# Sums over partitions with the stationary data in four column groups of 32

## The reference

```python
cs = jax.nn.silu(c)
for i in range(2):
    mod = (cs @ ada_w[i] + ada_b[i])[:, None, :]
    sh1, sc1, g1, sh2, sc2, g2 = jnp.split(mod, 6, axis=-1)
    h = rms_norm(x, norm1_g[i]) * (1.0 + sc1) + sh1
    x = x + g1 * mixer_i(h)          # 0: dilated attention, 1: S5 state space
    h = rms_norm(x, norm2_g[i]) * (1.0 + sc2) + sh2
    x = x + g2 * conv_ffn(h)
return rms_norm(x, final_norm_g)
```

## Time and profile before

| | |
|---|---|
| median of three runs | 2857.9 us |
| span of the profiled execution | 2854.5 us |
| TensorE busy with matmuls / weight loads | 97% / 88% |
| VectorE / ScalarE / GpSimd busy | 79% / 44% / 16% |
| mean granted TensorE clock | 0.985 |
| HBM traffic | 254 GB/s over the span |

### The profile page before, as it was taken

How to read it: one execution, slowest core, us unless ns; L and a number is a source line. 1 busy time by engine, 2 the same in 40 slices (tenths; PEclk the granted TensorE clock), 3 DMA queues, 4 the chain that set the end, 5 groups by cost and what they waited for, 6 DMA issues and landing times.

```text
span 2854.5 us, 52641 instructions
## 1 busy us (share of the span) xinstructions
PE 2761.2 (97%) x19980; PEld 2521.2 (88%) x19980; DVE 2249.6 (79%) x3003; ACT 1267.3 (44%) x1775; POOL 466.5 (16%) x461
## 2 busy tenths in 40 slices
PE   8799999999989999999999999989999999999998
PEld 3788888888889999999999998989878888888887
DVE  7887877777869988889888778987888875666655
ACT  1334444444434544434444334444355553455542
POOL 4061111011023111000111111234401110000121
PEclk9899999999999999999999999999999999999999
DMA  9989887787756888878888876768867766655563
GB/s 361 352 275 371 294 277 267 261 267 259 263 178 232 295 296 287 281 234 302 300 295 304 270 245 215 241 205 281 310 218 242 265 183 187 194 185 186 183 183 111
DMA packets 241693, 724.50 MB, mean 254 GB/s; under 512 B 50912, under 2 KB 59872, under 8 KB 240736
## 3 DMA queue, kind: packets, MB, share of 16 engines
q1 hardware_dynamic: 185184, 666.98, 68.9%
q10 hardware_dynamic: 56320, 54.93, 6.2%
HBM read 700.58 MB, written 25.43 MB: 254 GB/s over the span
## 4 chain that ended last, share of the span: by engine, by line
PE 87%; DVE 6%; issue 3%; DMA 2%; ACT 1%; POOL 1%; ACTq 0%; SPq 0%; DVEq 0%; POOLq 0%
PE proj L1827 31%; PE proj L1830 15%; PE proj L1832 11%; PE proj L1834 11%; PE proj L1833 11%; DVE acc L1025 2%; PE pmisc L1856 1%; PE proj L1826 1%; DMA raw<-in_w_in 1%; DMA ada<-in_ada_w 1%; DVE w_lo L1116 1%; PE ps L1915 1%; PE ps L1942 1%; PE proj L1915 1%; PE ps L2026 1%
## 5 line engine op out<-in xcount | busy, mean ns | idle before, releaser
L566 ACT ACTIVATE w_hi<-raw 128x1024 fp32r<-128x1024 f32 (+1 forms) x896 | 935.6, 1045 | 1411.3 <-PE proj L1834 580.0
L1116 DVE TENSOR_TENSOR w_lo<-raw,w_hi 128x1024 fp32r<-128x1024 f32 (+1 forms) x896 | 1107.1, 1236 | 467.1 <-ACT w_hi L566 462.3
L1827 PE MATMUL proj<-h_hl,w_hi 128*128 128x512 f32 x3232 | 1139.5, 400 | 6.5 <-DVE work L1294 3.9
L1830 PE MATMUL proj<-h_hl,w_lo 128*128 128x256 f32 x3030 | 851.5, 281 | 0.0
L1827 PEld LDWEIGHTS proj<-h_hl,w_hi 128*128 128x128 f32 x3232 | 599.0, 189 | 138.0 <-DVE work L1294 4.2
L1830 PEld LDWEIGHTS proj<-h_hl,w_lo 128*128 128x128 f32 x3030 | 574.6, 190 | 7.3
L1832 PE MATMUL proj<-h_hl,w_hi 128*128 128x256 f32 x1888 | 548.6, 291 | 30.0 <-DVE h_hl L1071 11.0
L1833 PE MATMUL proj<-h_hl,w_hi 128*128 128x256 f32 x1888 | 538.8, 285 | 0.0
L1834 PE MATMUL proj<-h_hl,w_lo 128*128 128x256 f32 x1888 | 538.6, 285 | 0.0
L1832 PEld LDWEIGHTS proj<-h_hl,w_hi 128*128 128x128 f32 x1888 | 366.1, 194 | 38.7 <-issue 12.7
L1025 DVE SCALAR_TENSOR_TENSOR acc<-ada,cs,acc 128x1024 f32<-128x1024 f32 x285 | 392.0, 1375 | 0.6 <-DMA ada<-in_ada_w 0.3
(11 more groups left out here) (259 smaller groups left out, 2441.9 us busy)
## 6 DMA issues: line engine op xcount, KB each, us to landing
raw<-in_w_up SPq DMA_DIRECT2D x352, 512.0 KB, 5.5
ada<-in_ada_w SPq DMA_DIRECT2D x348, 512.0 KB, 5.9
raw<-in_w_in SPq DMA_DIRECT2D x224, 512.0 KB, 5.8
raw<-in_w_down SPq DMA_DIRECT2D x128, 448.0 KB, 3.8
raw<-in_w_down SPq DMA_DIRECT2D x64, 512.0 KB, 3.8
raw<-in_w_out SPq DMA_DIRECT2D x32, 512.0 KB, 5.1
raw<-in_ssm_w_in SPq DMA_DIRECT2D x32, 512.0 KB, 4.9
raw<-in_ssm_w_gate SPq DMA_DIRECT2D x32, 512.0 KB, 5.7
```

What stands on the lines that cost most here:

```text
L566: nc.scalar.activation(w_hi[:, j % LAG, 0:nk * P], raw[:, j % s.ring, 0:nk * P], ACT.Copy).then_inc(hi_ready, 1)
L1116: V.tensor_tensor(w_lo[:, j % LAG, 0:nk * P], raw[:, j % s.ring, 0:nk * P], w_hi[:, j % LAG, 0:nk * P].bitcast(F32), ALU.subtract).then_in ...
L1827: ins = mm(both, w_hi[:, j % LAG, w], hl[:, k].rearrange("p c t -> p (c t)"), start=(k == 0), stop=end)
L1830: ins = mm(o, w_lo[:, j % LAG, w], hi[:, k, :], start=False, stop=False)
```

## The change

Each 128 x 128 stationary matrix of these sums is given in four parts of 128 x 32 columns, each with its own matmul on the same column of ones, and each writes 32 partitions of the same PSUM column. The values computed and where they land stay the same, and so do all waits and the one semaphore increment on the last matmul.

```diff
@@ sum_part @@
                 for c in range(MODB):
-                    ins = mm(mod_ps[:, c:c + 1], v[:, c * P:(c + 1) * P], ones[:, 0:1], start=True, stop=True)
+                    for q in range(4):
+                        ins = mm(mod_ps[32 * q:32 * q + 32, c:c + 1], v[:, c * P + 32 * q:c * P + 32 * q + 32], ones[:, 0:1],
+                                 start=True, stop=True)
                 ins.then_inc(mod_summed, 1)
@@ sum_early @@
                     for c in range(MODB):
-                        ins = mm(early_ps[n][:, c:c + 1], v[:, c * P:(c + 1) * P], ones[:, 0:1], start=True, stop=True)
+                        for q in range(4):
+                            ins = mm(early_ps[n][32 * q:32 * q + 32, c:c + 1], v[:, c * P + 32 * q:c * P + 32 * q + 32],
+                                     ones[:, 0:1], start=True, stop=True)
                     ins.then_inc(early_summed, 1)
```

## The result

The changed kernel takes 2838.5 us, the median of five runs (2837.1 to 2842.1), against 2857.9 us before (five runs, 2855.5 to 2859.6). The ratio is 0.9934, with a 95% interval of 0.9923 to 0.9944: 19.4 us less, where 10.9 us less was forecast. The profiled execution took 2840.84 us with a span of 2839.0 us, so 1.8 us lie around a span, and not the 3.4 us that stand in the prediction. The two spans differ by only 15.5 us, since the profiled execution of before was one of the quicker ones of its kernel (2854.5 + 1.8 = 2856.3 us) and that of after one of the slower ones.

A forecast was written before the change was run, and what follows sets the result against it. TensorE, 87% of the chain, was taken as the bound. A part falling from 1.79 to 1.24 us saves 0.55 us, over 21 parts 11.5 us, less 0.6 for VectorE 10.9: 2847.0 us, range 2841 to 2854.

The forecast's parts named there:

- The forecast case: Whole kernel: a gain between 5.7 and 15 us, with a chance of 0.74.
- term (a): In each part of the sums: 64 narrow pairs at 14.1 ns each, with bounds of 7 and 30 ns.
- Entry and exit: Around each part, between product matmuls: going into and out of the narrow shape costs 0.34 us.
- The 0.6 us taken off for VectorE: FFN streams, where `w_lo` from VectorE would be late next: about one part's gain lost, 11.5 to 10.9 us.
- the first early part is hidden: Near 115 us: a weight DMA of 15.55 us covers this part, so 21 of 22 parts count.
- The fast rival: Narrow pairs of the sums: faster than 14 ns; 2837 us at 7 ns, 2842 halfway; chance 0.10.
- The slow rival: Narrow pairs of the sums: loads run one after the other, 28 ns a pair, 2865 us; chance 0.06.
- The 3.4 us around the span: Outside the profiled span: 3.4 us added to the predicted span of 2843.6 us to give 2847.0 us.

The follow-up runs named there:

- the first three norms: Changed kernel with the sums of mean() also in four column groups, 32 pairs instead of 8 in each norm (16 instead of 4 in the first): 2835.4 us, ratio 0.9921.

## Why the prediction was wrong

- **The forecast case was right, its size wrong.** The sums were on the chain, the narrow pairs run side by side, and no wait takes the place of what is removed (TensorE waits 1.1 us for `w_lo` instead of 1.2): all as argued. The forecast time lay 8.5 us too high, and the measured one below the range.
- **The step that failed** is term (a), the pair at 14.1 ns. The prediction took it from rows with 63 moving columns because "only the moving width differs", and concluded that 14.1 "should not be exceeded". That bounds it from above alone, and the width was what set it. Measured: 8.6 ns with one column, 14.1 with 63. The difference, 5.5 ns x 64 pairs = 0.35 us a part, is 7.4 us over 21 parts, nearly all of the error.
- **Entry and exit** were 0.29 us instead of 0.34, 1 us in all.
- **The 0.6 us taken off for VectorE** weren't lost. The sum with the measured terms, 21 x 0.95 = 20 us, meets the measured 19.4 us. The doubled sums (12 to 13 us for 10.6 added) show no cover either. That the first early part is hidden rests on the chain alone: the run with only the early sums changed gave 1.1 us for both, too near to nothing to decide it.
- **The fast rival was the case**: a pair faster than 14 ns, 2837 us at 7 ns, with a chance of 0.10. Its lower end came from the right mechanism, four groups side by side at 28 / 4 = 7 ns. That 7 lies so near to 8.6 is in part luck, for with half of the columns the pair still costs 8.0 ns, so the load isn't what holds it. The chance was too small and the range stopped halfway to it. The trace of before could have decided it: a float32 pair over 256 moving columns costs 216 ns at full width, (1.46 - 0.38) / 5 in the line below, where 0.38 us is one record. So 63 columns cost 53 ns in a group, and four groups bring that to 13 ns. The 14.1 ns were explained by a term that the change doesn't have.

```profile
469.88 1.46 PE L1942 MATMUL ps<-work 128*128 128x256 f32 x6
```

- **The slow rival** (28 ns a pair, 2865 us) is what the same instructions do in another order: 27.3 ns and 2862.5 us.
- **The 3.4 us around the span** were 1.8 us; it doesn't touch the forecast, which goes by a difference.

## What to carry to other kernels

A sum over partitions with a one-column moving operand is bounded by the 128 stationary columns of its load; four column groups of 32, visited in turn, cut the run from 1.79 to 0.84 us, as long as the moving operand has fewer than some 40 columns (an estimate, 4 x 8.6 / 0.85; 32 cost next to nothing, 63 cost 0.4 us a part) and each matmul goes to another group than the last one. It helps only where the next step waits for the sum and not for another engine, as the first three norms show. When a price is taken from a row that differs in one size, work out first which size sets that row: if it is the one that differs, the row is a bound and not the price, and the range has to reach to the other bound.

## What the runs showed of the hardware

For float32 pairs, in one column group a pair costs about the larger of stationary columns x 0.85 ns and moving columns x 0.85 ns. Measured in one group alone are 27.3 ns for 32 stationary and 1 moving column and, at full width, 108 for 128 and 63. Worked out from groups that alternate are 2 x 29 = 58 for 64 and 1, 4 x 14.1 = 56 for 32 and 63, and 4 x 27.1 = 108 for 32 and 128. Groups that alternate share this out among them, down to a floor of 8.0 to 8.9 ns a pair. The Trainium skill, page "TensorE: Matmul & The Clock Gate", section "Back-to-back issue gap", gives some 60 cycles, about 25 ns, as the least distance for 1 to 64 moving columns; the rows here have 8.6 ns, so that isn't a floor across column groups. Going from full-width products to narrow sums and back costs about 0.29 us; full-width sums at the same place have 0.09 us beside their pairs.
